# Causal attention on one core: units of a group in descending length, mixes two steps behind their units, a second set of turned rows

## What is computed

```python
def fox_attention(q, k, v, log_f):                      # 8 heads, 512 tokens, head width 64
    s = einsum('bhqd,bhkd->bhqk', qi, k) * scale
    s = s + ci[..., :, None] - c[..., None, :]
    s = where(kpos[None, :] <= qpos[:, None], s, -inf)  # causal
    p = softmax(s)
    return einsum('bhqk,bhkd->bhqd', p, v)
...
    # the other 8 heads, for the three branches
    o_n = g[..., 0:1] * o_c + g[..., 1:2] * o_s + g[..., 2:3] * o_w
```

## Time and profile before

| | |
|---|---|
| median of three runs | 3250.35 us (3239.62 to 3250.83) |
| the profiled execution | 3251.51 us, span 3249.7 us |
| PE busy over the span | 3105.7 us, 96% |
| DVE, ACT, POOL busy | 48%, 32%, 7% |
| causal attention, layer 1 | from about 244 to 369 us |
| causal attention, layer 2 | from about 1029 to 1154 us |

### The profile page before, as it was taken

The page is one execution under the profiler, slowest core; times in us unless marked ns, Lnnn a source line. Parts: engine busy times, 40 slices in busy tenths (PEclk is TensorE's granted clock), DMA queues, the critical chain, the costliest instruction groups (busy, mean ns, idle before and its releaser), DMA issues. The chain is left out here.

```text
span 3249.7 us, 39408 instructions
## 1 busy us (share of the span) xinstructions
PE 3105.7 (96%) x15558; PEld 2096.5 (65%) x15558; DVE 1575.3 (48%) x2411; ACT 1046.1 (32%) x1660; POOL 236.9 (7%) x363
## 2 busy tenths in 40 slices
PE   8999999999999999999998999999979999999996
PEld 6884588888787478888785574454437457454442
DVE  5316658888523665888766461211126656121113
ACT  4326434444323624444443422000013543200002
POOL 1004200000101400000010200000000320000000
PEclk9999999999999999999998999999999999999998
DMA  6410233332440032333402148999992114999997
GB/s 176 131 41 27 78 105 102 103 102 53 127 146 27 1 104 78 104 104 104 119 8 68 52 157 369 421 414 422 422 375 66 59 65 176 377 421 412 422 422 311
DMA packets 229305, 590.71 MB, mean 182 GB/s; under 512 B 37830, under 2 KB 141068, under 8 KB 179996
## 3 DMA queue, kind: packets, MB, share of 16 engines
q1 hardware_dynamic: 229148, 588.52, 48.0%
HBM read 582.18 MB, written 2.10 MB: 180 GB/s over the span
## 5 line engine op out<-in xcount | busy, mean ns | idle before, releaser
L3077 PE MATMUL ps<-w_ring,xe 128*64 128x512 f32 x1024 | 229.8, 595 | 7.3 <-DMA w_ring<-in_w 5.0
L3077 PE MATMUL ps<-ex_front,xe 128*64 128x512 f32 x1024 | 232.9, 598 | 0.0
L3077 PE MATMUL ps<-ex_front,hidT 128*64 128x512 f32 x1024 | 226.0, 598 | 4.4 <-ACT hidT L3134 2.2
L1159 ACT ACTIVATE mlp_w_hi<-w_ring 128x2048 fp32r<-128x2048 f32 x86 | 165.3, 1926 | 187.7 <-PE ps L1096 71.9
L1261 DVE TENSOR_TENSOR mlp_w_lo<-w_ring,mlp_w_hi 128x2048 fp32r<-128x2048 f32 x86 | 196.6, 2288 | 43.4 <-ACT mlp_w_hi L1159 43.4
L361 PE MATMUL ps<-h_hi,in_w_hi 128*128 128x512 f32 (+1 forms) x528 | 207.2, 392 | 0.2 <-DVE h_lo L439 0.2
L361 PE MATMUL ps<-h_lo,in_w_hi 128*128 128x512 f32 (+1 forms) x528 | 205.8, 390 | 0.0
L361 PE MATMUL ps<-h_hi,in_w_lo 128*128 128x512 f32 (+1 forms) x528 | 205.7, 390 | 0.0
L1096 PE MATMUL ps<-h_hi,mlp_w_hi 128*128 128x512 f32 x512 | 199.8, 390 | 0.4 <-DVE h_lo L1367 0.4
L1096 PE MATMUL ps<-h_hi,mlp_w_lo 128*128 128x512 f32 x512 | 199.4, 389 | 0.0
L1096 PE MATMUL ps<-h_lo,mlp_w_hi 128*128 128x512 f32 x512 | 199.4, 389 | 0.0
(11 more groups left out here) (611 smaller groups left out, 6480.2 us busy)
## 6 DMA issues: line engine op xcount, KB each, us to landing
ex_front<-in_w SPq DMA_DIRECT2D x256, 1024.0 KB, 15.2
w_ring<-in_w SPq DMA_DIRECT2D x128, 1024.0 KB, 16.8
w_ring<-in_w_in SPq DMA_DIRECT2D x32, 1024.0 KB, 5.4
w_ring<-in_w_up SPq DMA_DIRECT2D x32, 1024.0 KB, 9.1
w_ring<-in_w_down SPq DMA_DIRECT2D x32, 1024.0 KB, 5.2
w_ring<-in_cmp_w SPq DMA_DIRECT2D x16, 512.0 KB, 4.8
w_ring<-in_w_out SPq DMA_DIRECT2D x8, 1024.0 KB, 6.0
w_ring<-in_w_o SPq DMA_DIRECT2D x8, 1024.0 KB, 8.5
```

Of the source, the lines that this page charges most:

```text
L1159: act.activation(w.hi[:, number(m, n) % HOMES, :], src, ACT.Copy).then_inc(s.hi_done, 1)
L3077: mm = pe.matmul(ps[rows, bank + half, :], lhsT, slot(2 * m + a)[:, kk, 512 * half:512 * half + 512], start=(k == 0), stop=(k == DC - 1))
```

## The change

The units of a causal group run i3, i2, i1, i0. Every mix has its own step, `mix_step(u)`. For groups 0 to 3 (units below `early` = 16) it stays seven steps behind, in the old order of key blocks. For units 16 and 17 it is six steps behind and from unit 18 on five, which is two steps behind the unit's flip; there the key block of the mix is the unit's own i, so the columns are 128, 256, 384, 512. `keep` follows one step behind the last mix of a bank as before (`keep_at`). `probsT` has two sets, and the takes wait for the mixes of two groups ago. DVE copies the two parts of i3 from the far end. The other attention kinds keep their order.

```diff
-    units = [(g, i) for g in range(len(groups)) for i in range(TT)]
+    order = range(TT - 1, -1, -1) if kind == "causal" else range(TT)
+    units = [(g, i) for g in range(len(groups)) for i in order]
...
+    early = TT * pieces.index(1) if kind == "causal" else nu
+
+    def mix_step(u):
+
+        return u + LAG + (TT if u < early else 3 if u < early + 2 else 2)
+    keep_at = {mix_step(TT * g + TT - 1) + 1: g for g in range(len(groups))}
...
-        sets = 1 if kind == "causal" else 2
+        sets = 2
...
-                def mix(g, kb):
-                    opens = g == 0 or closes(g - 1)
-                    if kb == 0:
-
-                        landed(pe, TT * g + TT - 1, 1)
+                def mix(u):
+                    g = u // TT
+                    kb = u % TT if u < early else units[u][1]
+                    opens, starts = g == 0 or closes(g - 1), u % TT == 0
+                    if u >= early:
+                        landed(pe, u, 1)
+                    elif starts:
+                        landed(pe, TT * g + TT - 1)
+                    if starts:
...
-                    if parts_of(TT * g + TT - 1) > 1 and kb == TT // 2:
-                        landed(pe, TT * g + TT - 1)
                     for a in range(2):
                         mm = pe.matmul(ps[64 * a:64 * a + 64, bank_of(g), q0:T], groups[g].v(a, kb), probsT[:, g % sets, a, kb, q0:T],
-                                       start=(opens and kb == 0 and not pieces[g]), stop=(closes(g) and kb == TT - 1))
+                                       start=(opens and starts and not pieces[g]), stop=(closes(g) and u % TT == TT - 1))
...
-                    u = step - LAG - 1 - (TT - 1)
-                    if 0 <= u < nu:
-                        mix(u // TT, u % TT)
+                    for u in range(nu):
+                        if mix_step(u) == step:
+                            mix(u)
...
-                        act.wait_ge(s.mixed, mixed_by[g - 1] - (TT - 1 - i) if kind == "causal" else mixed_by[g - 2])
+                        act.wait_ge(s.mixed, mixed_by[g - 2])
...
-                    u = step - LAG - 2 - (TT - 1)
-                    if u >= 0 and u % TT == TT - 1:
-                        keep(u // TT)
+                    if step in keep_at:
+                        keep(keep_at[step])
...
-                    for k in range(0, keys(i) // P, step):
+                    for k in range(keys(i) // P - step, -1, -step):
```

More of the change, by code:

```diff
@@ L799, in take @@
                     if g >= sets:
-                        dve.wait_ge(s.mixed, mixed_by[g - 1] - (TT - 1 - i) if kind == "causal" else mixed_by[g - 2])
+                        dve.wait_ge(s.mixed, mixed_by[g - 2])
                     dst, src = landing(g, i)
                     step = keys(i) // P // parts_of(u)
-                    for k in range(0, keys(i) // P, step):
+                    for k in range(keys(i) // P - step, -1, -step):
                         dve.tensor_copy(dst[:, :, k:k + step, :], src[:, :, k:k + step, :]).then_inc(s.copied_v, 1)
```

## The result

Ten runs each: the changed kernel has a median of 3263.54 us (3258.87 to 3278.82), the kernel before 3251.43 us (3239.62 to 3254.98). The recorded ratio is 1.005, with a 95% interval of 1.0035 to 1.0066 (the two medians alone would give 1.0037). The profiled execution took 3261.52 us, span 3259.7. Forecast were 3267.5 us and a range of 3255 to 3284.

What follows compares the result with a forecast made beforehand. PE was taken to bound the kernel, busy 116.1 of 125 us in the causal stretches. Per layer -0.3 + 3.1 + 8.2 - 2.5 = +8.5, in all +17.0 on 3251.5, less 1.2 to the median: 3267.5 us, range 3255 to 3284.

Steps and rivals of the forecast that it cites:

- Sort A and B: Alternating four-step periods in steps 27 to 47: with `keep` and piece 11.64 us, wait 2.1; without 9.44, wait 0.9.
- Late part: Steps 27 to 47 of each layer's causal attention: 53.8 us instead of 45.58, +8.2 a layer.
- Steps 7 to 27: Early part of each layer's stretch: PE waits for takes of i2 and i1 on ACT, +3.1 us.
- Head and end: Per layer: up to step 7, -0.3 us; from the last scores of i0 to the end, -2.5 us.
- Sum: All terms of the attention stretches together: +8.5 us a layer, +17.0 in all.
- Rival 1, the clock: PE's clock falls at the late `keep` waits, 1.5 to 3 us each, six times: +12, 3280; chance 0.25.
- Rival 2, half the size: The early part's waits don't come, +3.1 becomes +0.5 in both layers: 3262 us; chance 0.12.
- Rival 3, not slower: The late part's waits don't come, its chain being 2.1 us shorter: -2.3 a layer, 3246 us; chance 0.08.

Runs made afterwards that it cites:

- e1: Changed kernel with `keep` in the late part (groups 5, 7, 9) two steps later; median 3252.45 us, ratio 1.0007 to the kernel before.
- e9: Changed kernel with ACT taking i3 alone and DVE the other three; medians 3239.79 and, again, 3239.29 us, ratios 0.9966 and 0.9975 to before.
- e3: Changed kernel with ACT taking i0 and i3, DVE i1 and i2; median 3247.08 us, ratio 1.0001 to the kernel before.
- e4: Changed kernel with ACT taking i0 and i3, and late `keep` two steps later; median 3258.41 us, ratio 1.0025 to the kernel before.
- e7: Kernel before with two `probsT` sets, only first and last groups longest first, late mixes in the last; median 3251.32 us, ratio 1.0009.

## Why the prediction was right, and where not

- **Sort A and B.** 11.64 and 9.44 forecast, 11.59 and 9.41 measured; waits 2.1 and 0.9 forecast, 2.04 and 0.71 to 0.83 measured. e1 shows that the place of `keep` set the chain off, e9 that it cost PE only because the take of i1 stood at its end on ACT.
- **Late part.** +8.2 forecast, +9.6 measured in layer 1: 11.59, 11.04, 11.59, 9.41, 11.58. The one of 11.04 is a sort B with PE at half rate, 1.63 too long; without it +8.0, as in layer 2.
- **Steps 7 to 27.** +3.1 forecast, +3.5 measured (51.16 for 47.64): the coarse term was a little low in nearly every period (10.53, 10.07, 9.62, 11.10 and 9.84 for 9.9 and the 0.5 of the first mix, 9.9, 9.6, 10.9 and 10.0). The waits ahead of flip1 are 0.53 to 0.96.
- **Head and end.** Head -0.3 forecast, -0.8 and +0.3 measured in the two layers; end -2.5 forecast, -2.7 and -1.6 measured. The head's near hit hides something that I overlooked in the kernel before: there both heads have a wait of 2.3 us with PE at half rate behind it, so this flip of four blocks takes 1.09 us and the same flip later 0.66:

```profile
255.73 1.09 PE L640 MATMUL ps<-ident,w_ring 128*128 128x128 f32 x4 [2.32 <-DVE at_probsT L805]
```

In the changed kernel's layer 1 the head has no half rate, but longer waits (0.72, 1.79 and 1.59 us).
- **Sum.** +8.5 a layer forecast, +9.7 and +10.2 measured. Layer 2 has no slow sort B, but its end takes 10.10, with the clock halved in it. So the stretches missed by 2.9 us in all, and the clock makes 2.7 of it.
- **Rival 1, the clock.** I took "no fall". In fact it falls behind some of the 2.04 us waits and not behind others: behind two of six in the profile after (flip of eight blocks 1.83 at 327.74, 1.09 at 338.78; the other in the end of layer 2) and three of six in the repeat, where the stretch of layer 2 is 138.84. It cost 1.1 and 1.6 us in the one and up to 3.1 in the other (11.84 + 12.23 for the pair of 21.00), about my price of 1.5 to 3; "six times" was wrong. The wait of 2.32 us in the head of the kernel before was a second row for this rival, in the very stage that changes, and I didn't weigh it. The Trainium skill, "TensorE: Matmul & The Clock Gate", section "HAM oscillation — how this bites in real kernels", expects half rate only behind an idle gap longer than these; the rows here don't agree, and by them a wait of 2 us is a risk, not a fixed cost.
- **Rival 2, half the size.** Out: +3.5 where it had +0.5. Its ground, that the waits before were two of 0.17, holds for the late pairs only; in steps 7 to 27 there were three more of 0.42 and one of 0.21.
- **Rival 3, not slower.** Out: no link of the chain was shorter.
- **The assumption that failed** isn't among the terms: the sum was made against one profiled execution, as if all outside the stretches stayed. There 11.1 us went away. The predicted 3267.5 lies between the changed kernel's two levels, and the median came out 4 us below it because six of ten runs lay on the lower; the repeat's median, with two of seven there, was 4.9 above it. The chain and its terms were right; the closeness of the total is partly luck. By the forecast's own line of 0.5% for "slower", to which it gave 0.56, the ratio of 1.005 lies just on that line.

## What to carry to other kernels

Before units are reordered, write down for each engine what will stand ahead of each instruction that another engine waits for; here a take behind the longest exponentials cost 0.5 to 0.9 us every group, and a rarely run store in the wrong step 2.0 us each time, as long as a take that PE waits for stood behind it (e9), with all instructions unchanged. Move a take to the engine whose queue is short at that moment, and count every reader of its result (e3) before it is moved. Where runs fall on levels, compare level with level and stretch with stretch in the profile; a median can show a gain or hide a loss of 10 us that the edit's own place doesn't have.

## What the runs showed of the hardware

PE's half rate, 1.2 GHz, sets in behind some waits of 2.04 us and not behind others of the same length in the same profile, and likewise behind a wait of 3.06 us before and not behind one of 3.07 us after the change. How long it lasts differs too: about 3.4 us after the two 2.04 us waits in the profile after, 6.8 us after those in layer 2 of the repeat. In one place of the second block it is 23.9 us in seven profiles (before, e1, e3, e4, e7, e9, the repeat of the changed kernel), with PE busy nearly throughout, and 6.8 us in the other six; in the two profiles of e9 it makes the two levels. In the kernel before, the long stretch sets in where PE has come out of waits of 1.36, 1.03 and 3.90 us. Why an execution gets one or the other, and why e9 gets the short one more often, stays open: no run separates it from the time at which that place is reached.
